# Value shifts issued by SP and subtracted by VectorE, and a first normalization applied by a diagonal matrix, in a hybrid transformer kernel

## The chip, the cores and the metric

One core of one Trainium2 chip runs the whole kernel as one program. The metric is the device time of one execution in microseconds (us), the median of three runs.

## The reference, cut to what matters

The reference is two transformer layers one after the other on x of 512 tokens by 1024 features, all in float32. What the change touches is the start of the first layer and the values of its stick-breaking attention:

```python
def hybrid_layer(x, norm_pre, w_in, ...):
    h = rmsnorm(x, norm_pre)                      # x * rsqrt(mean(x*x) + EPS) * norm_pre
    proj = jnp.einsum('bld,de->ble', h, w_in)
    z_ssd, xbc, dt_raw, q, k, v, z_sb, gates = jnp.split(proj, _split_points(), axis=-1)
    # xbc: causal convolution of 4 taps, silu; dt: softplus; then ssd_scan (chunked scan)
    # y: gated group rmsnorm with z_ssd
    o = stick_breaking(q, k, v)                   # causal, 16 heads of 64
    ...

# stick_breaking, per block of queries
log_fail = jnp.where(mask, jax.nn.log_sigmoid(-logits), 0.0)
between = lax.cumsum(log_fail, axis=3, reverse=True) - log_fail
w = jnp.where(mask, jnp.exp(jax.nn.log_sigmoid(logits) + between), 0.0)
outs.append(jnp.einsum('bhqk,bkhd->bqhd', w, v[:, :kend]))
```

The second layer (sparse attention, a gated linear recurrence, a feed-forward network) follows and is not touched. The kernel doesn't form w itself: a reverse scan on VectorE gives running sums of weights, and these are multiplied with the steps of the values, v[t] - v[t-1], which gives the same output.

## The kernel before, in words

Tokens lie in four tiles of 128 (index t, `NT`), features in eight chunks of 128 (index k, `NK`). Every large product runs as three float32r products (high half of the weights times high half of the activations, and the two mixed ones). Weights come in blocks of up to 128x2048, each in two pieces of 128x1024 that SP loads (L699) into two buffers `wraw`; ScalarE rounds a piece to `whi` (`round_weights`, L1150), VectorE subtracts to get `wlo` (`rest_of_weights`, L1485). SP loads piece i of block n when `wlo` of piece i of block n-1 is done (L697). Every function of TensorE ends in `mm`, recorded as L744; transposes against the identity are recorded at their own lines.

`plan()` writes one list of steps, `STEPS`, and every engine walks it in that order and does its share of each step. So a wait of one instruction holds up everything behind it on that engine. Each block is a run of eight `gemm` steps; ScalarE rounds the next block's pieces at steps 0 and 2, VectorE makes the rests at steps 2 and 4.

**The start.** SP loads the four tiles of x (L692), the constants `cst` with the identity (L690) and, spread over all partitions, the weights `norm_pre` (L691). For each tile ScalarE squares and sums (`norm`, L1263), VectorE makes mean and reciprocal (L1637, L1638), ScalarE takes the root (`root`, L1244), VectorE multiplies the tile by its factor and `norm_pre` (`apply`, L1648), TensorE turns it in two halves of four transposes (`turn`, L807), ScalarE rounds each half out of PSUM into `a_hi` (L1267) and VectorE writes the rest to `a_lo` (L1680). Then comes the small product for dt (`small_block`, 16 products with `sw`), for which all splits must be done, and block 0 of the projection. The first block needs `whi` (L1150) and `wlo` (L1485) of its first piece; both engines make them after the last split of x.

**The convolution.** Blocks 0 to 5 give the twelve tiles of xbc. For each tile VectorE does four convolution instructions (`conv`, L1502 and L1504 three times) and a product (`silu`, L1515). Step `ssd_decay` comes after block 2: TensorE sums decays (two products of `stat` and `cst`), VectorE reads them (L1852 to L1856) and only then has TensorE a free bank for the next transposes (`xturn`, L1008). POOL begins that step with the zeroing of `rounded_arena` (L2011, 128x1024; it reads the identity, times 0.0), which VectorE waits for only at step `stack`, and then does `decays(0)` and `decays(1)` (two L2003 each), which wait for dt.

**The values.** Blocks v to v+3 (so the four value blocks are called here) give v in two halves of 512 features. When the last token tile of a half is summed, ScalarE copies it out (L1224) and issues three DMAs on its own queue (L1229 to L1231, 896 KB, 120 KB and 6 KB) that copy the half, shifted by one token, into `v_before`. POOL then subtracts (L2056, 128x2048) once for each half. In between the same two engines turn and round y for the group norm (steps `norm`, `apply` L1652, `turn` L807 and L1267 for y), which is woven into blocks v to v+2. Blocks v+4 and v+5 are the first two gate blocks; into these and the fourteen that follow the 64 units of stick-breaking are woven, one per `gemm` step. Unit u: logits on TensorE, two sigmoids on ScalarE (L1291, L1292), the scan on VectorE (L1926); two units later the transposes (L1085) and their copy (L1301), three later the product with the value steps (`bank<-arena`). The first unit's sigmoid waits for the first half of the steps (`s_dv` 1), heads from 8 on and the first `y_ssd` tile (L1543) for the second (`s_dv` 2).

The lines of the old value path:

```python
act.wait_ge(s_vz, half + 1)
act.dma_start(v_before[half][1:113, :, :], vt[0:112, :, cols]).then_inc(s_vs[half], 16)
act.dma_start(v_before[half][113:P, :, :], vt[112:P - 1, :, cols]).then_inc(s_vs[half], 16)
act.dma_start(v_before[half][0:1, 1:NT, :], vt[P - 1:P, 0:NT - 1, cols]).then_inc(s_vs[half], 16)
```

Of the kernel before, what the change touches and what calls it, by code (L numbers as in the profile page):

```python
# [23 lines left out]
ALU = mybir.AluOpType  # L24
# [7 lines left out]
P = 128  # L32
T = 512
D = 1024
# [46 lines left out]
def plan():  # L81
# [52 lines left out]
    for row in normed(["x"], gap=1):  # L134
        steps += row[::-1] if row[-1][0] != "turn" else row
# [118 lines left out]
def plan_tiles():  # L254
# [3 lines left out]
    for s in STEPS:  # L258
        if s[0] == "gemm":
            begun += opened(BLOCKS[s[1]], s[2])  # L260
            done += closed(BLOCKS[s[1]], s[2])
            ended += closed(BLOCKS[s[1]], s[2])
        elif s[0] in ("turn", "small", "smallturn", "qkturn", "level", "hout"):
# [18 lines left out]
    groups = {"turn": (4, 6, 7), "dt": (7,), "level": (2, 3), "hout": (2, 3), "turn_qk": (2, 3), "hq": (0, 1), "hf": (0, 1),  # L282
# [46 lines left out]
FILLS = {"x": "A", "y": "B", "mix": "A", "hgrn": "B", "ffn": "A"}  # L329
ROWS = {"x": "norm_pre", "y": "ssd_norm", "mix": "norm_mix", "ffn": "norm_ffn"}  # L330
# [8 lines left out]
def plan_splits():  # L339
# [9 lines left out]
    for s in STEPS:  # L349
        if s[0] == "turn":  # L350
            done(s, FILLS[s[1]], range(4 * s[3], 4 * s[3] + 4), [s[2]])
        if s[0] == "merge":
# [34 lines left out]
CST = Columns([("ident", P), ("tri", P), ("ones", P)])  # L387
# [16 lines left out]
TURNS = [s for s in SPLITS if s[0] in ("turn", "nsa")]  # L404


def block_of(kind):
    return min(n for n, b in enumerate(BLOCKS) if TILES[b["tiles"][0]][0] == kind)

# [11 lines left out]
def emit(nc, dram, spill, out):  # L421
    ctx = ExitStack()
    with ctx:
# [84 lines left out]
        vt = mem(32, [NT, D])  # L508
        junks = {"x": mem(0, [NT, D]), "y": mem(60, [2, 512])}
        rows = {"x": mem(64, [D]), "y": mem(48, [D]), "mix": mem(80, [D]), "ffn": mem(0, [D])}  # L510
# [100 lines left out]
        s_vz, s_dv = sem("s_before_first_zero"), sem("s_value_steps")  # L611
# [6 lines left out]
        s_out = sem("s_stored")  # L618
        s_hid4, s_hidz = sem("s_hidden_repeated"), sem("s_hidden_zero")
# [66 lines left out]
        def _(sp):  # L686
            by_token = lambda ap: ap.rearrange("(a p) d -> p a d", p=P)
            for t in range(NT):
                if t == 2:
                    sp.dma_start(cst[:, :], dram["cst"]).then_inc(s_ident, 16)  # L690
                    sp.dma_start(rows["x"], dram["norm_pre"]).then_inc(s_row["x"], 16)  # L691
                sp.dma_start(xt[:, t, :], by_token(dram["x"])[:, t, :]).then_inc(s_x[t], 16)  # L692
            sp.dma_start(swraw[:, 0:NK * SH], dram["w_dt"]).then_inc(s_sw, 16)
            for n in range(NB):
                for i in range(2):
# [3 lines left out]
                    sp.dma_start(wraw[i][:, 0:cols.stop - cols.start], dram["wblk"][n][:, cols]).then_inc(s_w[i], 16)  # L699
                if n == 1:  # L700
# [41 lines left out]
        def _(pe):  # L742
# [56 lines left out]
            def turn(name, t, half, g):  # L799
                src = {"x": xt, "y": xs, "mix": xn, "hgrn": mixt, "ffn": xn}[name]  # L800
# [1335 lines left out]
```

## Time and profile before

| | before |
|---|---|
| median of 3 runs | 1460.55 us (1459.8 to 1462.16) |
| profiled execution, its own time | 1462.84 us |
| its span | 1461.0 us |
| TensorE busy | 1390.3 us (95%) |
| VectorE busy | 757.8 us (52%) |
| ScalarE busy | 582.6 us (40%) |
| GpSimd busy | 121.2 us (8%) |
| mean DMA rate | 83 GB/s |
| mean granted TensorE clock | 0.985 |

The span is the time from the first to the last recorded instruction; 1.84 us lie around it. Busy time of overlapping matmuls is counted once. The chain that ended last lies on TensorE for 82%, on VectorE for 10% and on ScalarE for 4% of the span. A duration behind "xN" is that of N instructions together, so their pitch is that time divided by N.

### The profile page before, as it was taken

How to read it: one execution, taken by the hardware profiler on the slowest of the kernel's cores; microseconds unless marked ns; L12 is line 12 of the kernel's file. 1: busy time of each engine (PE TensorE's matmuls, PEld its weight loads, DVE VectorE, ACT ScalarE, POOL GpSimd, SP SyncE). 2: the span in 40 equal slices, each digit the busy share in tenths (PEclk: the TensorE clock that was granted, in tenths of full speed). 3: DMA queues.
4: the chain of work that ended last, by engine and by line, in shares of the span. 5: the costliest groups of instructions: out<-in, count | busy, mean ns of one | idle time of the engine just before them, and what ended most of it. 6: DMA issues, size and time to landing. Idle time of an engine off the chain costs nothing.

```text
span 1461.0 us, 17660 instructions
## 1 busy us (share of the span) xinstructions
PE 1390.3 (95%) x6909; PEld 1133.9 (78%) x6913; DVE 757.8 (52%) x1148; ACT 582.6 (40%) x1061; POOL 121.2 (8%) x87
## 2 busy tenths in 40 slices
PE   6899999998999999998899989999979999999999
PEld 4787778876888888876787767767868888888887
DVE  4775554555666553334554757557643433443443
ACT  4534333446777532234425444542332322322221
POOL 0107430011000000000000122221000000000000
PEclk9999999999999999999999999999999999999999
DMA  4221222332111254222431100000512233223322
GB/s 156 74 85 58 76 69 84 104 115 58 59 58 45 79 179 140 92 95 73 151 103 58 44 15 29 15 16 15 173 58 87 88 101 100 92 97 100 100 88 101
DMA packets 35493, 121.78 MB, mean 83 GB/s; under 512 B 3924, under 2 KB 5204, under 8 KB 35154
## 3 DMA queue, kind: packets, MB, share of 16 engines
q1 hardware_dynamic: 33744, 117.50, 24.0%
q10 hardware_dynamic: 1666, 3.14, 0.8%
q8 instruction: 56, 0.92, 0.2%
q14 instruction: 27, 0.22, 0.0%
HBM read 113.29 MB, written 4.19 MB: 80 GB/s over the span
## 4 chain that ended last, share of the span: by engine, by line
PE 82%; DVE 10%; ACT 4%; issue 2%; ACTq 1%; DMA 1%; POOL 0%; SPq 0%; DVEq 0%
PE bank L744 79%; PE bank L1085 1%; PE bank L906 1%; PE bank L807 1%; DVE wlo L1485 1%; DVE arena L1504 1%; ACT arena L1263 1%; DMA arena<-in_x 1%; ACT whi L1150 0%; DVE arena L1779 0%; DVE arena L1655 0%; DVE arena L1810 0%; ACT a_hi L1267 0%; DVE arena L1784 0%; DVE a_lo L1680 0%
## 5 line engine op out<-in xcount | busy, mean ns | idle before, releaser
L744 PE MATMUL bank<-a_hi,whi 128*128 128x512 f32 x848 | 342.2, 404 | 1.5 <-DVE arena L1933 0.9
L744 PE MATMUL bank<-a_hi,wlo 128*128 128x512 f32 x848 | 332.7, 392 | 0.0
L744 PE MATMUL bank<-a_lo,whi 128*128 128x512 f32 x848 | 332.3, 392 | 0.0
L1485 DVE TENSOR_TENSOR wlo<-wraw,whi 128x1024 fp32r<-128x1024 f32 x194 | 248.6, 1293 | 54.5 <-ACT whi L1150 49.1
L1150 ACT ACTIVATE whi<-wraw 128x1024 fp32r<-128x1024 f32 x194 | 196.9, 1044 | 183.2 <-PE bank L744 177.1
L744 PE MATMUL bank<-arena 128*128 128x128 f32 (+7 forms) x1400 | 221.0, 304 | 9.0 <-DVE arena L1784 4.9
L744 PEld LDWEIGHTS bank<-arena 128*128 128x128 f32 (+2 forms) x1400 | 175.4, 190 | 36.6 <-issue 21.3
L744 PEld LDWEIGHTS bank<-a_hi,wlo 128*128 128x128 f32 x848 | 160.4, 189 | 34.6
L744 PEld LDWEIGHTS bank<-a_hi,whi 128*128 128x128 f32 x848 | 160.8, 190 | 33.9 <-issue 2.0
L744 PEld LDWEIGHTS bank<-a_lo,whi 128*128 128x128 f32 x848 | 160.9, 190 | 31.9 <-issue 1.0
L744 PE MATMUL bank<-whi,a_hi 128*128 128x512 f32 x320 | 127.8, 400 | 6.9 <-DVE a_lo L1680 3.9
L744 PE MATMUL bank<-whi,a_lo 128*128 128x512 f32 x320 | 125.7, 393 | 0.0
L744 PE MATMUL bank<-wlo,a_hi 128*128 128x512 f32 x320 | 125.5, 392 | 0.0
L744 PE MATMUL bank<-whi,b_hi 128*128 128x512 f32 x240 | 94.5, 394 | 0.0
L744 PE MATMUL bank<-whi,b_lo 128*128 128x512 f32 x240 | 94.1, 392 | 0.0
L744 PE MATMUL bank<-wlo,b_hi 128*128 128x512 f32 x240 | 93.9, 391 | 0.0
L1926 DVE TENSOR_TENSOR_SCAN arena<-arena 128x128 f32<-128x128 f32 (+1 forms) x64 | 56.7, 888 | 67.1 <-ACT arena L1292 66.8
L744 PEld LDWEIGHTS bank<-whi,a_hi 128*128 128x128 f32 x320 | 60.6, 190 | 19.9 <-issue 7.7
L1199 ACT ACTIVATE b_hi<-arena 128x512 fp32r<-128x512 f32 x30 | 19.0, 632 | 135.6 <-DVE arena L1590 123.7
L744 PEld LDWEIGHTS bank<-whi,a_lo 128*128 128x128 f32 x320 | 60.6, 189 | 12.9
L744 PEld LDWEIGHTS bank<-wlo,a_hi 128*128 128x128 f32 x320 | 60.7, 190 | 11.9
L1580 DVE TENSOR_TENSOR arena<-arena,bank 128x512 f32<-128x512 f32 x32 | 22.0, 688 | 92.1 <-PE bank L744 92.1
(235 smaller groups left out, 1671.5 us busy)
## 6 DMA issues: line engine op xcount, KB each, us to landing
wraw<-in_wblk SPq DMA_DIRECT2D x190, 512.0 KB, 3.7
arena<-in_x SPq DMA_DIRECT2D x4, 512.0 KB, 6.0
arena<-in_x SPq DMA_DIRECT2D x1, 2048.0 KB, 8.3
spill<-arena SPq DMA_DIRECT2D x4, 512.0 KB, 6.6
arena<-spill SPq DMA_DIRECT2D x1, 2048.0 KB, 9.4
out<-arena SPq DMA_DIRECT2D x8, 256.0 KB, 2.6
arena<-arena ACTq DMA_DIRECT2D x2, 896.0 KB
arena<-in_w1k SPq DMA_DIRECT2D x1, 1024.0 KB, 7.1
```

The costliest lines, as they stand in the source:

```text
L744: return nc.tensor.matmul(o, lhsT, rhs, start=start, stop=stop, **kw)
L807: last = nc.tensor.transpose(bank[BANK[g]][:, P * i:P * i + P], src[:, t, c0 + P * i:c0 + P * i + P], ident)
L906: last = nc.tensor.transpose(bank[BANK_WT][:, o:o + P], np_[v % 3][:, b_, P * kb:P * kb + P], ident)
L1085: last = nc.tensor.transpose(bank[BANK_WT][:, P * kb:P * kb + P], sb_w[:, v % 3, P * kb:P * kb + P], ident)
L1150: A(whi[n % 2][:, cols], wraw[i][:, 0:cols.stop - cols.start], ACT.Copy).then_inc(s_hi, 1)
L1199: A(b_hi[:, c, :], tt[:, p % 2, :], ACT.Copy).then_inc(s_tround, 1)
L1263: A(junk[:, t, :], src[:, t, :], ACT.Square, accum_out=nss[name][:, t:t + 1]).then_inc(s_ss, 1)
L1485: v.tensor_tensor(wlo[n % 2][:, cols], wraw[i][:, 0:cols.stop - cols.start], f32(whi[n % 2][:, cols]), ALU.subtract).then_inc(s_lo, 1)
L1504: ins = v.scalar_tensor_tensor(acc[:, j:T], x_[:, 0:T - j], V("conv_w", 4 * i + 3 - j), acc[:, j:T], ALU.mult, ALU.add)
L1580: v.tensor_tensor(x, x, ps[:, :], ALU.add).then_inc(s_end["V"], 1)
L1926: v.tensor_tensor_scan(w[:, ::-1], fail[:, ::-1], sig[:, ::-1], 0.0, ALU.mult, ALU.add)\
```

## The change

At the start: `norm_pre` comes as eight columns of `cst`, which is loaded second. VectorE writes `diag`, the identity times the token factors of a tile (128x128), in place of the scaled tile. TensorE multiplies each 128x128 chunk of the raw x by `diag` as an ordinary float32 product (`feed`, eight a tile), which turns and scales it at once, into eight banks, one per feature chunk. After the fourth tile, ScalarE and VectorE split whole chunks of 128x512 (step `chunk`), with `norm_pre` as scale per partition. `small_block` waits chunk by chunk. Before all that, TensorE does 14 products of a constant, and ScalarE takes a root of a constant. On POOL, `decays(0)` comes before the zeroing. In the value path SP issues the shifting DMAs, between the two pieces of blocks v+4 (first half) and v+5 (second half), and VectorE subtracts in four instructions of 128x512 for each half: the first half at step `stack`, the second one by one in units 4 to 7. Cut to its core:

```diff
-    for row in normed(["x"], gap=1):
-        steps += row[::-1] if row[-1][0] != "turn" else row
+    chunks = [tile("x_t", c) for c in range(NK)]
+    for t in range(NT):
+        steps += [("norm", "x", t), ("apply", "x", t), ("feed", t)]
+    steps += [("chunk", c, g) for c, g in enumerate(chunks)]
...
-            need[s[:2]] = max(v for (x, _, _), v in last.items() if x == "A")
+            for k in range(NK):
+                need[(*s[:2], k)] = max(last["A", t, k] for t in range(NT))
...
-CST = Columns([("ident", P), ("tri", P), ("ones", P)])
+CST = Columns([("ident", P), ("tri", P), ("ones", P), ("norm_pre", NK)])
+WARMING = 14
+SHIFTS = [block_of("v") + 4, block_of("v") + 5]
...
             for t in range(NT):
-                if t == 2:
+                if t == 1:
                     sp.dma_start(cst[:, :], dram["cst"]).then_inc(s_ident, 16)
-                    sp.dma_start(rows["x"], dram["norm_pre"]).then_inc(s_row["x"], 16)
...
+                    if i == 0 and n in SHIFTS:
+                        half = SHIFTS.index(n)
+                        src, dst = vt[:, :, 512 * half:512 * half + 512], v_before[half]
+                        sp.wait_ge(*ended(tile_of("v", (NT - 1, half))))
+                        sp.wait_ge(s_y, NT)
+                        if half == 1:
+                            sp.wait_ge(s_split, max(SPLITS.index(x) for x in SPLITS if x[:2] == ("turn", "y")) + 1)
+                        sp.dma_start(dst[1:113, :, :], src[0:112, :, :]).then_inc(s_vs[half], 16)
+                        sp.dma_start(dst[113:P, :, :], src[112:P - 1, :, :]).then_inc(s_vs[half], 16)
+                        sp.dma_start(dst[0:1, 1:NT, :], src[P - 1:P, 0:NT - 1, :]).then_inc(s_vs[half], 16)
...
+            def feed(t):
+                if t == 0:
+                    pe.wait_ge(s_warm, 1)
+                    for _ in range(WARMING):
+                        mm(bank[NK - 1][:, T - P:T], warm, warm, True, True)
+                pe.wait_ge(s_norm, norm_no("x", t))
+                for c in range(NK):
+                    last = mm(bank[c][:, P * t:P * t + P], xt[:, t, P * c:P * c + P], diag[:, t, :], True, True)
+                    if t == NT - 1:
+                        last.then_inc(s_tile, 1)
...
-                need_split(SPLIT_NEED["small", kind])
                 for k in range(NK):
+                    need_split(SPLIT_NEED["small", kind, k])
...
-                    if t == NT - 1:
-                        ... (the three act.dma_start of before, with their waits)
...
+            act.wait_ge(s_unit, 1)
+            A(unit_root, unit, ACT.Sqrt)
             for s in STEPS:
-                if s == ("apply", "x", NT - 1):
+                if s == ("chunk", 0, tile_of("x_t", 0)):
                     round_small("dt")
...
+                if s[0] == "chunk":
+                    c, g = s[1:]
+                    act.wait_ge(s_tile, DONE[g])
+                    A(a_hi[:, c, :], bank[BANK[g]][:, :], ACT.Copy, scale=cst[:, CST.at("norm_pre")][:, c:c + 1]).then_inc(s_round, 1)
...
-                    last = v.scalar_tensor_tensor(xt[:, t, :], xt[:, t, :], r, rows["x"], ALU.mult, ALU.mult)
+                    dve.wait_ge(s_ident, 16)
+                    last = v.tensor_scalar(diag[:, t, :], ident, r, None, ALU.mult)
...
+            def steps_of_values(half, t):
+                cols = slice(512 * half, 512 * half + 512)
+                dve.wait_ge(s_vs[half], 48)
+                ins = v.tensor_tensor(vt[:, t, cols], vt[:, t, cols], v_before[half][:, t, :], ALU.subtract)
+                if t == NT - 1:
+                    ins.then_inc(s_dv, 1)
             def stick(u):
+                if NT <= u < 2 * NT:
+                    steps_of_values(1, u - NT)
...
+            v.memset(unit, 1.0).then_inc(s_unit, 1)
+            v.memset(warm, 1.0).then_inc(s_warm, 1)
             for s in STEPS:
+                if s[0] == "chunk":
+                    c, g = s[1:]
+                    dve.wait_ge(s_round, TURNS.index(s) + 1)
+                    v.scalar_tensor_tensor(a_lo[:, c, :], bank[BANK[g]][:, :], cst[:, CST.at("norm_pre")][:, c:c + 1],
+                                           f32(a_hi[:, c, :]), ALU.mult, ALU.subtract).then_inc(s_split, 1)
...
+                    for half in range(2):
+                        link(v.memset(v_before[half][0:1, 0, :], 0.0))
+                    for t in range(NT):
+                        steps_of_values(0, t)
...
                 if s[0] == "ssd_decay":
+                    decays(0)
                     pool.wait_ge(s_ident, 16)
                     g_.tensor_scalar(mem(92, [2 * NT, P], rounded_arena), ident.unsqueeze(1).to_broadcast([P, 2 * NT, P]), 0.0, None,
                                      ALU.mult).then_inc(s_kz, 1)
-                    decays(0)
...
-                if s[0] == "stack":
-                    ... (POOL's memsets of v_before and its two subtractions, L2052 and L2056)
```

## Rows read from the trace of the kernel before

**Rows 1.** Busy time in stretches: stretch, length, busy of each engine, PEclk, DMA

```profile
62.00:74.00 12.00, 6.83 (x26) 5.53 (x26) 7.10 (x14) 5.92 (x10) 0.00 (x0) 0.72 0.23 72
...
326.00:347.00 21.00, 14.06 (x59) 10.74 (x59) 11.78 (x10) 11.16 (x22) 4.52 (x1) 0.84 0.35 101
```

**Rows 2.** Timeline of ScalarE at the start: start, duration, instruction, idle before

```profile
4.48 1.06 ACT L1263 ACTIVATE arena<-arena 128x1024 f32<-128x1024 f32 x1 [2.46 <-DMA arena<-in_x]
...
6.92 1.28 ACT L1244 ACT_TABLE_LOAD   x1
...
9.97 1.06 ACT L1263 ACTIVATE arena<-arena 128x1024 f32<-128x1024 f32 x1 [1.55 <-DMA arena<-in_x]
...
20.50 1.99 ACT L1150 ACTIVATE whi<-wraw 128x1024 fp32r<-128x1024 f32 x2
```

**Rows 3.** Timeline of VectorE at the start

```profile
8.77 1.29 DVE L1648 SCALAR_TENSOR_TENSOR arena<-arena,stat 128x1024 f32<-128x1024 f32 x1 [1.49 <-DMA arena<-in_norm_pre]
...
21.58 2.36 DVE L1485 TENSOR_TENSOR wlo<-wraw,whi 128x1024 fp32r<-128x1024 f32 x2 [0.25 <-ACT whi L1150]
```

**Rows 4.** Timeline of TensorE at the start

```profile
10.11 1.97 PE L807 MATMUL bank<-cst,arena 128*128 128x128 f32 x8 [10.11 <-DVE arena L1648]
...
27.03 0.40 PE L744 MATMUL bank<-a_hi,whi 128*128 128x512 f32 x1
```

**Rows 5.** Timeline of GpSimd: the zeroing, and the second subtraction

```profile
6.61 2.77 POOL L2011 TENSOR_SCALAR rounded_arena<-cst 128x1024 fp32r<-128x1024 f32 x1 [6.17 <-DMA cst<-in_cst]
...
335.14 4.52 POOL L2056 TENSOR_TENSOR arena<-arena 128x2048 f32<-128x2048 f32 x1 [14.24 <-DMA arena<-arena]
```

**Rows 6.** Timeline of TensorE after the stall at 62.8 us

```profile
67.99 1.08 PE L1008 MATMUL bank<-cst,arena 128*128 128x128 f32 x4 [5.17 <-DVEq L1856]
```

**Rows 7.** Timeline of VectorE in the convolution, beside GpSimd's products and after them

```profile
53.15 4.30 DVE L1504 SCALAR_TENSOR_TENSOR arena<-arena,vec 128x511 f32<-128x511 f32 x3
...
59.68 2.33 DVE L1504 SCALAR_TENSOR_TENSOR arena<-arena,vec 128x511 f32<-128x511 f32 x3
```

**Rows 8.** Timeline of ScalarE and its queue around the two halves of the values

```profile
303.94 1.57 ACTq L1231 DMA_DIRECT2D arena<-arena  x1
...
328.98 1.95 ACTq L1231 DMA_DIRECT2D arena<-arena  x1
...
332.63 0.28 ACT L1291 ACTIVATE arena<-bank 128x128 f32<-128x128 f32 x1
...
337.73 1.06 ACT L1150 ACTIVATE whi<-wraw 128x1024 fp32r<-128x1024 f32 x1
```

**Rows 9.** Timeline of TensorE around the values and the first units

```profile
311.90 0.66 PE L807 MATMUL bank<-cst,arena 128*128 128x128 f32 x4 [1.75 <-DVE arena L1652]
...
340.26 0.69 PE L1085 MATMUL bank<-cst,arena 128*128 128x128 f32 x2 [4.05 <-DVE arena L1926]
...
345.54 0.77 PE L744 MATMUL bank<-b_hi,whi 128*128 128x512 f32 x1
...
350.73 1.06 PE L744 MATMUL bank<-arena 128*128 128x128 f32 x8
351.54 0.48 PE L744 MATMUL bank<-b_hi,whi 128*128 128x512 f32 x1
```

**Rows 10.** Timeline of VectorE around the values and the first units

```profile
299.08 1.41 DVE L1652 SCALAR_TENSOR_TENSOR arena<-arena,stat 128x512 f32<-128x512 f32 x2 [1.22 <-ACT stat L1244]
...
316.97 5.02 DVE L1485 TENSOR_TENSOR wlo<-wraw,whi 128x1024 fp32r<-128x1024 f32 x1 [1.23 <-ACT whi L1150]
...
335.39 5.67 DVE L1926 TENSOR_TENSOR_SCAN arena<-arena 128x256 f32<-128x256 f32 x2 [0.94 <-ACT arena L1292]
```

**Rows 11.** SP's weight loads before unit 0, and their time to landing

```profile
322.02 3.99 SPq L699 DMA_DIRECT2D wraw<-in_wblk  x2
...
DMA to landing us min/median/max: 3.0/3.7/9.8
```

**Rows 12.** DMA queues from 326 to 346 us: packets, MB, share

```profile
q10 hardware_dynamic: 545, 1.05, 20.2%
```

More of the change, by code:

```diff
@@ L262, in plan_tiles @@
             ended += closed(BLOCKS[s[1]], s[2])
+        elif s == ("feed", 0):
+            begun += [g for g, (kind, _) in enumerate(TILES) if kind == "x_t"]
+        elif s[0] == "chunk":
+            done.append(s[2])
+            end[s[2]] = ("split", s)
         elif s[0] in ("turn", "small", "smallturn", "qkturn", "level", "hout"):
@@ L280, in plan_tiles @@
     bank, before = {}, {}
-    groups = {"turn": (4, 6, 7), "dt": (7,), "level": (2, 3), "hout": (2, 3), "turn_qk": (2, 3), "hq": (0, 1), "hf": (0, 1),
+    groups = {"x_t": (0, 1, 2, 3, 4, 5, 6, 7), "turn": (4, 6, 7), "dt": (7,), "level": (2, 3), "hout": (2, 3), "turn_qk": (2, 3), "hq": (0, 1), "hf": (0, 1),
               "gate": (0, 1, 2), "y_ssd": (0, 1, 2)}
@@ L351, in plan_splits @@
             done(s, FILLS[s[1]], range(4 * s[3], 4 * s[3] + 4), [s[2]])
-        if s[0] == "merge":
+        if s[0] in ("merge", "chunk"):
             done(s, "A", [s[1]])
@@ L403 @@
 MERGE_AFTER = max(n for n, b in enumerate(BLOCKS) if b["w"] == "gate_sb")
-TURNS = [s for s in SPLITS if s[0] in ("turn", "nsa")]
+TURNS = [s for s in SPLITS if s[0] in ("turn", "nsa", "chunk")]
 def block_of(kind):
     return min(n for n, b in enumerate(BLOCKS) if TILES[b["tiles"][0]][0] == kind)
+SHIFTS = [block_of("v") + 4, block_of("v") + 5]
 def end_of(kind, i=None):
@@ L508, in emit @@
         vt = mem(32, [NT, D])
+        diag = mem(64, [NT, P])
+        warm = mem(66, [P])
+        unit, unit_root = stat[:, STAT - 2:STAT - 1], stat[:, STAT - 1:STAT]
         junks = {"x": mem(0, [NT, D]), "y": mem(60, [2, 512])}
-        rows = {"x": mem(64, [D]), "y": mem(48, [D]), "mix": mem(80, [D]), "ffn": mem(0, [D])}
+        rows = {"y": mem(48, [D]), "mix": mem(80, [D]), "ffn": mem(0, [D])}
         craw = mem(0, [2, T])
@@ L1105, in _ @@
                     turn(*s[1:])
+                if s[0] == "feed":
+                    feed(s[1])
                 if s[0] == "small":
@@ L2092, in lay_out @@
     cst[:, CST.at("ones")] = 1.0
+    cst[:, CST.at("norm_pre")] = cols(norm_pre[0])
     bf = mybir.dt.np(BF16)
@@ L2118, in lay_out @@
             "w1v": w1(cmp_v_w1_2), "cst2": cst2, "upto": upto, "cmask": cmask.reshape(P, P),
-            "halves": halves.reshape(P, 6 * 256), "onorm": rows(hgrn_o_norm_2[0]), "norm_pre": rows(norm_pre[0]),
+            "halves": halves.reshape(P, 6 * 256), "onorm": rows(hgrn_o_norm_2[0]),
             "ssd_norm": rows(ssd_norm[0]), "norm_mix": rows(norm_mix_2[0]), "norm_ffn": rows(norm_ffn_2[0])}
```

30 lines of the change are left out of this document (6 added, 24 removed).

## The prediction, made before the changed kernel was run

> **What bounds the kernel now.** I read the chain of waits first: it lies on TensorE nearly throughout, so only stretches in which TensorE waits can give time back. The waits listed by engine and the busy time by stretch then show where: 10.11 us before its first transposes [rows 4] and the slow build-up behind them; a stall at 62.8 us, where it is busy for 6.83 of 12 us; and 326 to 347 us, where it is busy for 14.06 of 21 us at a mean clock of 0.84 [rows 1]. The timelines of each engine in those three places do the rest. Everything between is matmul after matmul, and a shift of its start shifts it whole. Sums stand against one profiled execution (1462.84 us, span 1461.0); the median is 2.29 us lower, and I take the differences over to it.
>
> **The start.** Before, ScalarE squares the first tile at 4.48, loads the root's table for 1.28 us at 6.92 and waits 1.55 us for the third tile, whose data comes behind 512 KB of `norm_pre` [rows 2]. Block 0 starts at 27.03 [rows 4], because after the last split of x come the small products, and because TensorE worked at the lower level: eight transposes took 1.97 us, 0.25 each, where four at granted clock 1.00 later took 0.66, 0.17 with their tail [rows 4, 9].
>
> After, step by step. A tile costs ScalarE square (1.06), reading the sum (about 0.1 more), VectorE's two short instructions and the root (estimated together 0.6 with their hand-overs from the spacing of this timeline), so 1.8 us. The table load goes before the data: 0 on the path. The 512 KB row transfer goes too: between the landings of the first and third tile, 4.48 and 9.97 [rows 2], came 0.2 MB of `cst` and three times 0.52 MB, so 0.32 MB/us, and 0.52 MB are 1.6 us: the third tile is there at 8.4. So factors are ready at 6.3, 8.1, 10.2 and 12.0; `diag` of 128x128 adds an estimated 0.25 us, which is 1.29/8 for an eighth of L1648's elements [rows 3] and 0.1 of fixed part (bounds 0.1 and 0.4). Feeds: a float32 product of 128x128 is two records; x8 took 0.81 us from its start to the next start (350.73 to 351.54 [rows 9]), so 0.20 us a product and 1.6 us a tile at the upper level, 3.2 us at the lower. Fourteen products of the constant from about 1.1 us last 5.6 us at the lower level, to 6.7, just when the first `diag` is there: they cost 0 or a few tenths, and their cover is the wait for x. I take the upper level for the feeds, as TensorE has then worked for over 5 us, while after the stall at 68 it was back up by the end of the stretch at mean 0.72 [rows 1]. Last feed 12.35 to 14.0, first chunk at 12.6. Then eight chunks: ScalarE 0.5 each, VectorE's scalar_tensor_tensor 1.41/2 = 0.70 each [rows 10]: it bounds, from 13.2 to 18.8. The 16 small products run in its shadow, two a chunk. `wlo` of piece one takes 2.36/2 = 1.18 [rows 3], so block 0 starts at 20.0 in place of 27.03: **gain 7.0**. Were TensorE at the lower level throughout, feeds would end at 19.9, the chunks at 21.4, the small products (0.40 each) at 25: gain 2. Both ends are kept.
>
> The Trainium skill (TensorE: Matmul & The Clock Gate, Terms) says that transpose mode is 4x faster for FP32 than a plain product. The rows at the upper level give at most 0.17 for a transpose and 0.20 for a product, so this trace disagrees; by the page a feed would take 8 x 4 x 0.11 = 3.5 us by estimate, block 0 would start about 3 us later, and this gain would be 4.
>
> **POOL's order.** `decays(0)` and (1) slow VectorE: three convolution instructions took 4.30 us beside them and 2.33 alone [rows 7]. That lag ends in TensorE's 5.17 us wait at 67.99 for VectorE's read of the decays [rows 6], since VectorE has no gap between. The zeroing took 2.77 us at 6.61 [rows 5], away from all that; now it runs between `decays(0)` and (1), inside this stretch. Waiting for it: `decays(1)` behind it on POOL (not needed before the scan's second unit, far later), and VectorE only at `stack`. Its price is what it takes from VectorE. Lower end 0: VectorE's L1648 started at 8.77, while the zeroing ran until 9.38, and took 1.29 for 1024 elements [rows 3, 5], no more for each than L1652 far from any GpSimd work, 0.70 for 512 [rows 10]. Upper end: all 2.77 us. The nearest row is the same instruction beside the same kind of VectorE work, but it shows only 0.6 of the 2.77 us; I **charge 0.7**.
>
> The Trainium skill (SBUF — State Buffer, Who interferes with whom) says that a VectorE instruction with two SBUF inputs contends with a GpSimd instruction that reads SBUF, and the second fully blocks. By it L1648 should have stretched by 0.6 us, which the row doesn't show; by it the price here would be near 2.8.
>
> **The values, first half.** ScalarE's three issues end at 303.94 + 1.57 = 305.51 [rows 8], 3.8 us after they began. Behind them stand the copy of a y turn, two roundings and the squares of the last y tile, so VectorE's L1652 is late and TensorE waits 1.75 us at 311.90 [rows 9]. Without them all of that comes 3.8 us earlier: **gain 1.75**, the clock was 1.00 and gives nothing. SP issues these DMAs after the `wlo` rest of block v+3's first piece, about 305, with 0.4 to 2 us each as on ScalarE's queue; behind them on SP only the second piece of v+4 waits, about 3 us, and it has over 10. POOL's first subtraction blocked VectorE's L1485 for 5.02 instead of 1.2 [rows 10], but 9 us before use: nothing.
>
> **The values, second half, and the first units.** Before: last value copy ends 327.3; three issues until 330.93 [rows 8]; table load; first sigmoid 332.63 [rows 8]. Then the scans of units 1 and 2 take 5.67 us beside POOL's second subtraction, which alone lasts 4.52 [rows 5, 10], and TensorE waits 4.05 at 340.26 and works at the lower level until about 346 [rows 9].
>
> After: VectorE at `stack` adds two tiny memsets and four subtractions at 1.18/2 = 0.6 each, about 3.1 us from about 324.4, where the timeline has its last work of that step, ending at 327.5; ScalarE's table load ends at 328.6 and hides them. If that cover went they would cost as much as they last past it. First sigmoid 328.65, 4.0 earlier. The same ladder of ScalarE that took 332.63 to 337.73 [rows 8] then asks for the second piece of block v+5 at 333.75. That is the new wait. SP now holds that load: it waits for the last value tile (327.3) and issues the shifts for 3.6 us, so the load goes out at 331.0, where it went at 322.02 + 3.99 - 0.33 = 325.7 [rows 11]. With a landing time of 3.7 [rows 11], and behind 1.05 MB of shifts [rows 12], I put it at 334.8. Queued behind that rounding are unit 3's sigmoids and unit 1's copy; TensorE waits for them at unit 4, some 2 us. VectorE's four subtractions of the second half, 0.6 each in units 4 to 7, fall into gaps of about 1 us a unit. TensorE starts unit 4's block step at 338.2 where it did at 345.54 [rows 9]: **gain 7.3**. Ends: without any wait its work from 327.5 takes about 8 us, 335.4, gain 10.1; if the piece lands 4 us later than I put it, 3.3.
>
> **Sum.** 7.0 + 1.75 + 7.3 - 0.7 = 15.35 us. Profiled execution 1447.5, median 1460.55 - 15.35 = **1445.2**. The dropped ACT, POOL and DMA work elsewhere hides behind TensorE and is worth nothing.
>
> **Rivals.**
> (a) The start gives little: TensorE isn't brought up, or the feeds run at the lower level, or a product costs the page's ratio. For it: no row shows what wakes the engine from the very start. Against: 5.6 us of products. Gain 2 to 4 in place of 7: 1449 to 1450.
> (b) The zeroing blocks VectorE whole, and `decays(1)` collides later as before: 2.1 us more than charged, 1447.3. The page's rule above speaks for it, the row at 8.77 against it.
> (c) SP becomes the bound at v+5: the piece lands 4 us later, so unit 3 and all behind it wait, and the clock stays down as it did for the 5 us before 346: 1449 to 1451, and 1452 with (b).
> (d) Slower than before: the same place, but SP's chain goes wrong by more. SP holds all loads in order; while it waits for the last value tile and issues, block v+5's second piece and all of v+6 stand behind it. From 15.35 us of further delay past 334.8, which is a landing after 350, the whole gain is gone and with 4 more us the time is 1464.5. For it: issues on this path took up to 1.95 us [rows 8] and landing up to 9.8 [rows 11]. Against: even these together give 5 us.
> (e) TensorE has no stall to give back, since VectorE or ScalarE's own ladder takes the place: start 2, values 1, zeroing 2.8 lost: 1460.
>
> **Chances.** Forecast 0.50, better than it (no waits in the units, gain up to 10) 0.12, (a) 0.14, (b) 0.10, (c) 0.08, (e) 0.04, (d) 0.02. Their times lie from about 1440.5 to 1452 but for the last two, so the range is **1440.5 to 1452**: at best 1445.2 - 2.8 (no wait in the units) - 0.7 (zeroing free) - 1 (start), at worst (a) or (c) together with (b). A measurement here can tell 0.2%, 2.9 us, from no change. Faster by more: 0.94; within: 0.04; slower: 0.02.
>
> **What the changed profile would show.** Right: block 0's first product near 20.0; feeds of 1.6 us; no table load between squares and root; VectorE's convolution near 47 to 53 longer by under 1 us and TensorE's wait at the decays 5 to 6 us; no wait above 0.5 us at the y turns; scans without POOL beside them; one wait of about 2 us near unit 4, released by ScalarE and behind it by a load of SP. Wrong: feeds of 3 us, a decay wait near 8 us, or a load of v+5 landing more than 10 us after the last value copy.

## The result and the profile after

The changed kernel takes 1449.21 us (median of 4 runs, 1447.66 to 1450.59) against 1461.36 us (4 runs, 1459.8 to 1462.55): ratio 0.9917, 95% interval 0.9900 to 0.9934, so 12.1 us or 0.83% faster. In a second set on another chip it took 1449.36 against 1461.59 us, ratio 0.9918 (0.9903 to 0.9933). The forecast was 1445.2 us in a range of 1440.5 to 1452. Each experiment below but the last two is a single execution, and executions of one kernel lie up to 3.5 us apart. The profiled execution took 1450.34 us with a span of 1448.5.

Line numbers moved: TensorE's `mm` is now L769, the squares L1293, the roots L1274, `diag` L1685, the chunk's two halves L1446 and L1987, `wlo` L1521, the convolution L1538 and L1540, `xturn` L1043, the shifts L722 to L724, the value steps L1954, the sigmoids L1321 and L1322, the scan L1972.

Busy time of the changed kernel in the three places (stretch, length, PE, PEld, DVE, ACT, POOL, PEclk, DMA; compare [rows 1]):

```profile
0.00:30.00 30.00, 27.43 (x147) 21.41 (x148) 12.49 (x28) 16.69 (x29) 0.20 (x4) 1.00 0.49 168
...
54.00:66.00 12.00, 5.94 (x28) 4.96 (x27) 9.08 (x17) 5.25 (x10) 0.55 (x1) 0.79 0.31 88
...
318.00:335.00 17.00, 13.67 (x78) 10.90 (x77) 12.66 (x20) 11.70 (x25) 0.00 (x0) 1.00 0.42 124
```

The stretch at the decays is no better than before (5.94 us busy of 12, where it was 6.83). The units' stretch is 17 us in place of 21, with the clock at 1.00 in place of 0.84.

The start, ScalarE (answers to [rows 2]):

```profile
0.73 1.28 ACT L1403 ACT_TABLE_LOAD   x1 [0.73 <-PEq L2173]
...
4.71 1.06 ACT L1293 ACTIVATE arena<-arena 128x1024 f32<-128x1024 f32 x1 [2.48 <-DMA arena<-in_x]
...
7.46 1.06 ACT L1293 ACTIVATE arena<-arena 128x1024 f32<-128x1024 f32 x1 [0.99 <-DMA arena<-in_x]
...
9.14 1.04 ACT L1293 ACTIVATE arena<-arena 128x1024 f32<-128x1024 f32 x1
...
10.80 1.04 ACT L1293 ACTIVATE arena<-arena 128x1024 f32<-128x1024 f32 x1
```

Now the second tile is the one waited for (7.46 us); the third and fourth are not. From there a tile costs 1.66 us. TensorE, same stretch (answers to [rows 4]):

```profile
1.08 7.82 PE L769 MATMUL bank<-arena 128*128 128x128 f32 x44 [1.08 <-DVE arena L1982]
9.61 5.62 PE L769 MATMUL bank<-arena 128*128 128x128 f32 x48 [0.70 <-DVE arena L1685]
...
21.22 0.47 PE L769 MATMUL bank<-a_hi,whi 128*128 128x512 f32 x1 [0.53 <-issue]
```

The first row holds the 14 products of the constant (28 records) and the first feed (16), the second the other three feeds, which run back to back: their 24 products start between 9.61 and 14.96, 0.22 us each, so a feed takes 1.8 us. Block 0 starts at 21.22 in place of 27.03.

The convolution beside GpSimd (VectorE, then GpSimd; answers to [rows 5, 7]):

```profile
47.43 3.64 DVE L1540 SCALAR_TENSOR_TENSOR arena<-arena,vec 128x511 f32<-128x511 f32 x3
...
51.59 2.06 DVE L1521 TENSOR_TENSOR wlo<-wraw,whi 128x1024 fp32r<-128x1024 f32 x1
53.58 1.26 DVE L1538 TENSOR_SCALAR arena<-arena,vec 128x512 f32<-128x512 f32 x1
```

```profile
48.27 3.21 POOL L2069 TENSOR_SCALAR rounded_arena<-cst 128x1024 fp32r<-128x1024 f32 x1
51.45 1.12 POOL L2060 TENSOR_TENSOR b_hi<-cst,b_hi 128x512 fp32r<-128x512 f32 x1
```

TensorE's longest waits in all of the changed kernel (who, for whom, total, times, longest; the second answers to [rows 6]):

```profile
PE bank L830 <- DVE arena L1692: 13.3, 5, 5.4
PE bank L1043 <- DVEq L1893: 6.1, 1, 6.1
```

The first units: ScalarE, then TensorE (answer to [rows 8, 9]):

```profile
321.33 1.28 ACT L1321 ACT_TABLE_LOAD   x1 [1.00 <-DVE arena L1954]
322.62 0.28 ACT L1321 ACTIVATE arena<-bank 128x128 f32<-128x128 f32 x1
...
329.05 1.06 ACT L1187 ACTIVATE whi<-wraw 128x1024 fp32r<-128x1024 f32 x1 [1.34 <-DMA wraw<-in_wblk]
```

```profile
327.85 0.41 PE L1120 MATMUL bank<-cst,arena 128*128 128x128 f32 x2 [1.15 <-DVE arena L1972]
...
331.49 0.52 PE L1120 MATMUL bank<-cst,arena 128*128 128x128 f32 x3 [1.29 <-ACT arena L1331]
...
332.21 0.48 PE L769 MATMUL bank<-b_hi,whi 128*128 128x512 f32 x1
```

Five marks on TensorE split the 12.5 us by which the span fell. They are used for all experiments: block 0's first product; the first `xturn` behind the decay wait; unit 0's first logits product; unit 4's block step; the end.

| | before | after | gained |
|---|---|---|---|
| start to block 0 | 27.03 | 21.22 | 5.8 |
| to the end of the decay wait | 40.96 | 41.95 | -1.0 |
| to unit 0 | 259.55 | 257.41 | 2.1 |
| to unit 4's block step | 18.00 | 11.63 | 6.4 |
| to the end | 1115.5 | 1116.3 | -0.8 |

### The profile page after: what moved, and what is told of

Same layout as the page of the kernel before. It is cut to its first block, busy times and chain, and to the rows that moved or that the text cites. A ratio compares the mean times of both kernels' runs of the same rounds, so it can differ in the third digit from the quotient of the medians.

```text
span 1448.5 us, 17782 instructions
## 1 busy us (share of the span) xinstructions
PE 1393.3 (96%) x6969; PEld 1138.4 (79%) x6973; DVE 753.4 (52%) x1160; ACT 581.5 (40%) x1061; POOL 111.6 (8%) x83
## 4 chain that ended last, share of the span: by engine, by line
PE 85%; DVE 8%; ACT 3%; issue 2%; DMA 1%; SPq 0%; DVEq 0%; ACTq 0%
PE bank L769 82%; PE bank L1120 1%; PE bank L941 1%; PE bank L830 1%; DVE wlo L1521 1%; ACT arena L1293 0%; DVE arena L1816 0%; DVE arena L1847 0%; DMA arena<-in_x 0%; DVE arena L1692 0%; DMA wraw<-in_wblk 0%; DVE arena L1821 0%; DVE arena L1826 0%; ACT whi L1187 0%; PE bank L1043 0%
## 5 line engine op out<-in xcount | busy, mean ns | idle before, releaser
L769 PE MATMUL bank<-a_hi,whi 128*128 128x512 f32 x848 | 341.9, 403 | 2.1 <-DVE arena L1979 0.9
L769 PE MATMUL bank<-a_hi,wlo 128*128 128x512 f32 x848 | 332.6, 392 | 0.0
L769 PE MATMUL bank<-a_lo,whi 128*128 128x512 f32 x848 | 332.0, 392 | 0.0
L1521 DVE TENSOR_TENSOR wlo<-wraw,whi 128x1024 fp32r<-128x1024 f32 x194 | 245.6, 1278 | 55.0 <-ACT whi L1187 49.6
L769 PE MATMUL bank<-arena 128*128 128x128 f32 (+8 forms) x1492 | 232.4, 303 | 10.8 <-DVE arena L1821 4.9
L769 PEld LDWEIGHTS bank<-arena 128*128 128x128 f32 (+2 forms) x1492 | 186.4, 191 | 38.8 <-issue 21.3
L769 PEld LDWEIGHTS bank<-a_hi,whi 128*128 128x128 f32 x848 | 160.7, 190 | 34.6 <-ACT whi L1187 2.0
L769 PEld LDWEIGHTS bank<-a_hi,wlo 128*128 128x128 f32 x848 | 160.1, 189 | 34.4
L769 PEld LDWEIGHTS bank<-a_lo,whi 128*128 128x128 f32 x848 | 160.7, 189 | 31.6 <-issue 1.0
L769 PE MATMUL bank<-whi,a_hi 128*128 128x512 f32 x320 | 128.5, 402 | 7.0 <-DVE a_lo L1717 3.9
L769 PE MATMUL bank<-whi,a_lo 128*128 128x512 f32 x320 | 126.5, 395 | 0.0
L769 PE MATMUL bank<-wlo,a_hi 128*128 128x512 f32 x320 | 126.2, 394 | 0.0
L769 PE MATMUL bank<-whi,b_hi 128*128 128x512 f32 x240 | 94.9, 395 | 0.0
L769 PE MATMUL bank<-whi,b_lo 128*128 128x512 f32 x240 | 94.2, 393 | 0.0
L769 PE MATMUL bank<-wlo,b_hi 128*128 128x512 f32 x240 | 94.2, 392 | 0.0
L1972 DVE TENSOR_TENSOR_SCAN arena<-arena 128x128 f32<-128x128 f32 (+1 forms) x64 | 52.7, 823 | 58.4 <-ACT arena L1322 58.2
L769 PEld LDWEIGHTS bank<-whi,a_hi 128*128 128x128 f32 x320 | 61.1, 191 | 20.0 <-issue 7.8
L769 PEld LDWEIGHTS bank<-whi,a_lo 128*128 128x128 f32 x320 | 60.9, 190 | 13.1
L769 PEld LDWEIGHTS bank<-wlo,a_hi 128*128 128x128 f32 x320 | 61.2, 191 | 12.1
```

The source lines that it names most:

```text
L769: return nc.tensor.matmul(o, lhsT, rhs, start=start, stop=stop, **kw)
L1521: v.tensor_tensor(wlo[n % 2][:, cols], wraw[i][:, 0:cols.stop - cols.start], f32(whi[n % 2][:, cols]), ALU.subtract).then_inc(s_lo, 1)
L1972: v.tensor_tensor_scan(w[:, ::-1], fail[:, ::-1], sig[:, ::-1], 0.0, ALU.mult, ALU.add)\
```

## The experiments

Traces are compared by these marks, since a single time scatters by about 1.5 us for the reason given further down. The marks scatter too: where the start is the changed kernel's, with the same loads in the same order, block 0 begins between 20.73 and 21.86 us (8 traces), because the second tile of x lands at different times. Experiments start from the changed kernel unless another is named. The expectations of experiments 1 and 2 count 19.3 and 12.9 us to unit 4's block step from the last value product, which starts 1.3 us before the mark at unit 0 (18.0 and 11.6).

**1. The value path alone, on the kernel before.**

```diff
 (kernel before)
+ SHIFTS, SP's block of waits and three dma_start, steps_of_values on VectorE
- the three act.dma_start, GpSimd's memsets and subtractions
```

> The kernel before with the value path alone changed (SP issues the shifts, VectorE subtracts). Theory, that the change is three separate gains which add up: block 0 stays at 27.0 us, TensorE's wait at the y turns (1.75 us) goes, and from the last value product to unit 4's block step it is 12.9 us as in the changed kernel, not 19.3; in all 8.3 us shorter, span near 1452.7. Rival, that the value path gains less at the old, slower start because the waits are where they are for other reasons: under 6 us.

Measured: 1452.75 us beside 1459.96, span 1451.0. Block 0 at 27.20, decay wait 5.16; from block 0 to unit 0 298.8 us instead of 300.5; to unit 4's block step 11.43 instead of 18.00. The gain up to that step is 8.1 us, where the theory has 8.3; the rival is out.

**2. The start alone** (the old value path and GpSimd's old order).

```diff
-                    decays(0)                      # ahead of the zeroing
+                    decays(0)                      # behind it, as before
- SP's shifts, VectorE's steps_of_values
+ the three act.dma_start, GpSimd's memsets and subtractions
```

> The changed kernel with the old value path (ScalarE issues, GpSimd subtracts) and GpSimd's old order. Theory of separate gains: block 0 at 21.2 us, the wait for the decays back near 5.2, the whole 5.8 us shorter, span near 1455.2, with the y wait of 1.75 us and 19.3 us up to unit 4's block step back. Rival, that part of the 5.8 us is lost again in the convolution whatever GpSimd does: the products after the decay wait come only 4.8 us early.

Measured: 1456.73 us, span 1454.9. Block 0 at 20.73, decay wait 5.20 with its end at 61.75, 6.24 us earlier than before: nothing is lost in the convolution, so the rival is out. The y wait is back (1.60 us), as is the long wait for the scans (3.60 us) and 16.6 us up to unit 4's block step. Two sizes missed: the start gains 6.3 us here and not 5.8, as the second tile came early (its squares at 6.73), and the last stretch is 1.4 us shorter than the 18.0 expected. TensorE was at the lower level for a shorter part of it: the granted clock was 0.82, 0.50 and 0.83 in the three stretches of 2 us from 332 us on, where the kernel before had 0.89, 0.50, 0.50 and 0.50 in the four from 338 us on.

**3. GpSimd's order alone undone.**

```diff
                 if s[0] == "ssd_decay":
-                    decays(0)
                     pool.wait_ge(s_ident, 16)
                     g_.tensor_scalar(...).then_inc(s_kz, 1)
+                    decays(0)
```

> The changed kernel with the zeroing ahead of decays(0) on GpSimd, as before. Theory, that the zeroing between the decays takes about 1 us from VectorE: the wait at the decays falls from 6.1 to 5.2 us and the products behind it start 1 us earlier, 62.2 instead of 63.2; if it now collides with VectorE's small work on diag at 6 to 9 us, block 0 moves by at most 0.3. Rival, that the extra wait comes from VectorE's own order after the faster start: it stays at 6 us.

VectorE and GpSimd of this kernel:

```profile
47.48 4.30 DVE L1540 SCALAR_TENSOR_TENSOR arena<-arena,vec 128x511 f32<-128x511 f32 x3
51.70 0.68 DVE L1551 TENSOR_TENSOR arena<-arena 128x512 f32<-128x512 f32 x1
52.30 1.21 DVE L1521 TENSOR_TENSOR wlo<-wraw,whi 128x1024 fp32r<-128x1024 f32 x1
```

```profile
5.30 2.77 POOL L2068 TENSOR_SCALAR rounded_arena<-cst 128x1024 fp32r<-128x1024 f32 x1 [4.86 <-DMA cst<-in_cst]
```

The decay wait is 5.17 us, and its end comes 41.04 us after block 0 instead of 41.95: 0.9 us. Block 0 stays (21.27). The zeroing between the decays costs 0.9 us of its 3.2. The rows say where. In the changed kernel the second of the three convolution instructions, started 0.6 us into the zeroing, took 1.41 us, and the third, started 2.1 us into it, 0.75 (alone each takes 0.75, beside the decays 1.41). That is 0.66 us. The rest is that `decays(1)`, pushed back, slows the weights' rest (2.06 for 1.21 us) and the next convolution instruction (1.26 for 0.53) in place of two convolution instructions. The single time of 1449.95 us shows nothing of it.

**4. Only the issuing back on ScalarE; 5. only the subtracting back on GpSimd.**

```diff
 (4) - SP's waits and three dma_start     + the three act.dma_start
 (5) - steps_of_values, VectorE's memsets + GpSimd's memsets and subtractions
```

> The changed kernel with the shifting DMAs issued by ScalarE again; VectorE subtracts. Theory, that issuing and subtracting each have their own price: the y wait of 1.75 us returns, the first sigmoid comes about 2 us later than in the changed kernel, since 3.6 us of issuing replace 1.6 us of waiting for the subtractions, and ScalarE's 1.34 us wait for the second piece of block v+5 goes; in all 3 to 4 us longer than the changed kernel. Rival, that the collision of GpSimd with the scans was the whole of it: no more than 2 us longer.

> The changed kernel with both subtractions (and the clearing of the first row) back on GpSimd; SP issues. Theory: the first sigmoid comes earlier than in the changed kernel by the 1 us that ScalarE waits there for VectorE; but the second subtraction then runs beside scans 1 to 3 and blocks VectorE for about 4 us, and TensorE's granted clock falls again. Unit 4's block step 3 to 5 us later. Rival, that the issues were the price and GpSimd's subtraction is harmless when it comes early: equal within 1 us.

| from unit 0 to unit 4's block step | VectorE subtracts | GpSimd subtracts |
|---|---|---|
| SP issues | 11.6 (after) | 12.3 (5) |
| ScalarE issues | 14.6 (4) | 16.6 (2), 18.0 (before) |

In (4) the y wait is back at 1.72 us, and the first sigmoid comes at 326.70, so 5.0 us after unit 0's logits product against 2.0 in the changed kernel. The mark at unit 4 comes 4.1 us later than in the changed kernel, the end of this one execution (1451.89 us) 2.7 us later. So issuing on ScalarE brings back the y wait of 1.7 us and lengthens the units by 3.0 us, and the first theory holds in its parts. Not all of the 3.0 is issuing: TensorE now waits 1.8 and 1.6 us there and then works at the lower level, which the changed kernel doesn't (the granted clock, third number from the right, is 0.61 and 0.54 where the changed kernel has 1.00):

```profile
332.00:334.00 2.00, 2.00 (x8) 1.70 (x9) 1.75 (x3) 2.00 (x4) 0.00 (x0) 0.61 0.13 16
334.00:336.00 2.00, 2.00 (x10) 1.73 (x9) 1.68 (x2) 0.94 (x4) 0.00 (x0) 0.54 0.74 240
```

By estimate from these two rows, (0.39 + 0.46) x 2 us, up to 1.7 us of the 3.0 is clock. In (5), 1452.1 us, the second subtraction does collide:

```profile
329.39 4.83 POOL L2108 TENSOR_TENSOR arena<-arena 128x2048 f32<-128x2048 f32 x1 [12.45 <-DMA arena<-arena]
```

```profile
332.30 3.33 DVE L1970 TENSOR_TENSOR_SCAN arena<-arena 128x512 f32<-128x512 f32 x2 [2.46 <-ACT arena L1322]
```

(the two scans take 1.65 us without it), but now at units 3 and 4, and unit 4's block step comes 0.6 us later after unit 0, not 3 to 5. That expectation missed, and the number is the rival's (equal within 1 us), though the subtraction was not harmless to VectorE: with early issues it meets a stretch in which TensorE waits for a weight piece anyway (2.2 us in one piece, with the granted clock at 0.65 and 0.50 in the two stretches of 2 us from 332 us on). What it costs behind that mark was not taken apart.

**6. No products of the constant.** The 14 products are left out (their result is never used).

```diff
-WARMING = 14
+WARMING = 0
```

> The changed kernel without the 14 products of a constant. They are 0 of the output. Theory, that they bring the feeds to the upper level: without them the first feeds take 3.2 us instead of 1.6 and TensorE, working from 6.8 us on, comes up during the second or third; the last feed then ends 0 to 2.5 us later, and block 0 starts up to 2 us later. Rival, that the 14 products give nothing, since the feeds wait for factors and the chunks are bound by VectorE: block 0 within 0.3 us of 21.2. Second rival, that they are in the way (the first feed starts late in the changed kernel): block 0 earlier.

TensorE, the four feeds:

```profile
6.67 9.42 PE L769 MATMUL bank<-arena 128*128 128x128 f32 x64 [6.67 <-DVE arena L1685]
```

From 6.67 to 10.86 us a record starts every 0.21 us, from 11.02 us on every 0.11, as in the changed kernel from 6.5 us on. The slower figure is double the other, which is the ratio of the two levels, 1.2 and 2.4 GHz; the granted clock in the profile says 1.00 in both, so in the first microseconds it has to be read from the pitch. The last tile's squares start 0.1 us later than in the changed kernel, the first chunk's copy at 14.57 in place of 13.71: the products give 0.75 us. Block 0 at 22.08 is above all traces with the products, if by only 0.2 us above the latest of them, whose second tile came 0.5 us later than here; both rivals are out.

**7. The root's table loaded late.**

```diff
-            act.wait_ge(s_unit, 1)
-            A(unit_root, unit, ACT.Sqrt)
```

> The changed kernel without the root of a constant at the start, so the root's table is loaded between the first squares and the first root. Theory: the load of 1.28 us falls into ScalarE's 0.99 us wait for the second tile of x, so it costs only about 0.5 us at block 0. Rival, that the load is on the path in full: block 0 1.3 us later.

```profile
5.51 1.28 ACT L1274 ACT_TABLE_LOAD   x1
6.92 1.04 ACT L1293 ACTIVATE arena<-arena 128x1024 f32<-128x1024 f32 x1
```

Block 0 at 20.79, 0.4 us earlier than in the changed kernel, time 1447.35. The load lies in the wait for the second tile, which happened to land by 6.92 here; in nine traces with the constants ahead of it and the early load its squares started between 6.73 and 8.09, eight of them at 7.42 or later. So the whole start tells nothing of the load's price, and both expectations missed. The rows tell a little: the load puts the first `diag` at 7.05 where it came at 6.51, the four feeds then run back to back from 7.39,

```profile
7.39 7.41 PE L769 MATMUL bank<-arena 128*128 128x128 f32 x64 [0.21 <-DVE arena L1683]
```

and the last of them starts 0.3 us after its `diag` is there. In this order of loads the early root is worth a few tenths at most. In the order of experiment 8, where the second tile's squares start at 6.05, the load would end at 6.8 by this trace; that was not run.

**8. The constants behind the second tile.**

```diff
-                if t == 1:
+                if t == 2:
                     sp.dma_start(cst[:, :], dram["cst"]).then_inc(s_ident, 16)
```

> The changed kernel with the constants loaded third, behind the second tile of x, in place of second. Theory, that block 0 is late against the forecast because the second tile lands at 7.5 to 8.1 us behind the constants: its squares start near 6.3 to 6.9 and block 0 starts 0.5 to 1 us earlier, while the first feed, which now waits for the identity, still ends before the second diag is ready. Rival, that the third and fourth tile bound it then: block 0 within 0.3 us of 21.2.

```profile
6.05 1.04 ACT L1293 ACTIVATE arena<-arena 128x1024 f32<-128x1024 f32 x1
8.37 1.06 ACT L1293 ACTIVATE arena<-arena 128x1024 f32<-128x1024 f32 x1 [0.57 <-DMA arena<-in_x]
```

The second tile isn't waited for any more, the third comes at 8.37, and block 0 starts at 20.34: 0.9 us earlier than in the changed kernel's first trace and 0.4 us earlier than in the best of the eight traces with its order. Time 1448.95.

**9. The second shift behind the second piece of block v+5.**

```diff
-                    if i == 0 and n in SHIFTS:
+                    if (n, i) in ((SHIFTS[0], 0), (SHIFTS[1], 1)):
```

> The changed kernel with the second half's shift issued after the second piece of block v+5 in place of before it. Theory: ScalarE's 1.34 us wait for that piece goes, and TensorE's 1.29 us wait at unit 4 with it; the shifts land before VectorE's unit 4, so unit 4's block step starts 1 to 1.5 us earlier. Rival, that VectorE waits at unit 4 for the shifts instead: nothing gained, or up to 1 us lost.

```profile
328.01 1.06 ACT L1187 ACTIVATE whi<-wraw 128x1024 fp32r<-128x1024 f32 x1
```

```profile
331.76 0.69 DVE L1954 TENSOR_TENSOR arena<-arena 128x512 f32<-128x512 f32 x1 [0.46 <-DMA arena<-arena]
```

ScalarE's wait and TensorE's at unit 4 are gone, VectorE waits 0.46 us for the shift, and the mark is at 10.32 instead of 11.63: 1.3 us, with the granted clock at 1.00 in both. Time 1447.0.

**10. The units' tables and rows ready.**

```diff
+  (ScalarE, unit 0) A(unit_root, unit, ACT.Sigmoid)   # ahead of its waits
-  (VectorE) link(v.memset(v_before[half][0:1, 0, :], 0.0))
+  (GpSimd) the same two memsets, early; VectorE waits for them
```

> The changed kernel with the first rows of v_before cleared by GpSimd early, and with a sigmoid of a constant on ScalarE ahead of its wait for the first value steps. Theory, that the table load of 1.28 us sits behind a wait of 1.0 us that hides nothing and that the two clearings with their hand-overs (1.28 us) make VectorE late: the first sigmoid comes 1.0 us after the last value copy starts to be free, about 1.3 to 1.6 us earlier than in the changed kernel. TensorE then still waits for the second piece of block v+5, so unit 4's block step moves by 0.3 us at most. Rival, that the first sigmoid alone sets it: unit 4 earlier by over 1 us.

The first sigmoid comes 1.17 us after unit 0's logits product instead of 2.04. But all of it, and more, goes into the next wait:

```profile
329.50 1.06 ACT L1187 ACTIVATE whi<-wraw 128x1024 fp32r<-128x1024 f32 x1 [2.16 <-DMA wraw<-in_wblk]
```

```profile
331.95 0.87 PE L1120 MATMUL bank<-cst,arena 128*128 128x128 f32 x3 [2.11 <-ACT arena L1333]
...
334.32 0.63 PE L769 MATMUL bank<-b_hi,wlo 128*128 128x512 f32 x1
```

Two waits of 1.15 and 1.29 us became one of 2.11, after which the products run at 0.43 us spacing in place of 0.23, the lower level, for some 3 us. Unit 4's block step is 0.6 us later (12.22), which neither the theory (0.3 us earlier at most) nor the rival had; the clock was left out of both. 1451.13 us.

**11 and 12. All mended, beside the changed kernel.** Experiments 3, 8, 9 and 10 together, and the changed kernel unedited.

> The changed kernel with four things mended: the zeroing ahead of decays(0), the second shift behind the second piece of block v+5, the constants behind the second tile of x, the first rows cleared by GpSimd and the sigmoid's table loaded ahead of the wait. Theory, that the losses are separate: 0.9 + 1.0 + 0.6 + 1.3 us, so 3 to 4 us under the changed kernel, near 1445.5. Rival, that the waits are shared and the last one stays: under 1.5 us.

> The changed kernel itself, unedited, beside the one with all four mended and on the same chip. Both theories: 1449.2 us, 0.8% under the kernel before. From the first units on its products take between 1113 and 1117 us in the traces so far, by how often the granted clock falls at short waits, so its times spread by some 3 us.

1444.28 us (4 runs, 1443.65 to 1446.08), ratio to the kernel before 0.9884 (0.9868 to 0.9901); the changed kernel beside it 1449.36, 0.9918 (0.9903 to 0.9933). The intervals just don't overlap: by the medians the mended one is 5.1 us faster than the changed kernel, more than the 3 to 4 expected, and 17.3 us faster than the kernel before. Up to unit 4's block step its trace is 4.1 us ahead of the changed kernel's first one (328.15 against 332.21) and 3.7 us ahead of that of experiment 12 (331.81); what is over lies behind that step, in the stretch that scatters. The 4.1 are 0.9 at the decays, 2.2 in the units, where no wait above 0.3 us is left after unit 0's logits, 0.9 between them, and only 0.1 at the start. The 0.9 between them belong to no edit but to the clock: in the 6 us behind the decay wait the granted clock was 0.61 in the changed kernel and 0.77 here, and a difference of 0.16 over 6 us is 1.0 us.

```profile
63.17:69.17 6.00, 6.00 (x19) 4.95 (x20) 1.45 (x2) 3.50 (x7) 0.00 (x0) 0.61 0.15 51
```

```profile
62.21:68.21 6.00, 6.00 (x23) 5.06 (x24) 1.45 (x2) 3.50 (x7) 0.00 (x0) 0.77 0.15 47
```

At the start the zeroing met the first `diag`. VectorE, GpSimd and TensorE:

```profile
6.61 1.09 DVE L1687 TENSOR_SCALAR arena<-cst,stat 128x128 f32<-128x128 f32 x1 [0.65 <-DMA cst<-in_cst]
```

```profile
6.58 2.83 POOL L2069 TENSOR_SCALAR rounded_arena<-cst 128x1024 fp32r<-128x1024 f32 x1 [6.14 <-DMA cst<-in_cst]
```

```profile
7.75 7.41 PE L769 MATMUL bank<-arena 128*128 128x128 f32 x64 [0.49 <-DVE arena L1687]
```

1.09 us where the three other tiles take 0.29. Both start on the landing of the constants. The four feeds then run back to back from 7.75 (6.74 in experiment 8), so the first one's delay reaches block 0 nearly whole: 21.16 against 20.34. Moving the zeroing to a place where neither stands in its way was not tried.

## Why the prediction was right, and where its sizes were off

The forecast of 15.35 us became 12.1: mechanism, places and order were right, and the range held. The time alone would not say so, since 1449.2 us is also what rivals (a) and (c) gave; it is the marks that rule these two out.

**The start, 7.0 forecast, 5.8 measured.** The term that was mis-sized most is the landing of the tiles. I took 1.6 us off for the row transfer that goes, and checked the third tile; but the change also moves 0.2 MB of constants ahead of the second tile, and I let its factor be ready at 8.1 as if it were there. It was at 9.2, and the two tiles behind it queued on ScalarE, so the last `diag` was ready at 12.9 and not at 12.25. The second term is the feed: I read x8 in 0.81 us as 0.20 us a product, but its eight records start 0.11 us apart, a product takes 0.22 and a feed 1.8 us, not 1.6. That is longer than the 1.66 us a tile, so three feeds back to back end up behind their factors, and the last one starts at 13.3, 0.4 us after its `diag`. Experiment 8 takes the late landing away, and with it most of that queue, and gives 20.34, near the 20.0 of the sum. The other terms held: 1.66 us a tile for 1.8; `diag` 0.29 for 0.25; 0.67 us a chunk (4.69/7) for 0.70. A float32 product's 0.22 us stands against 0.11 for a transpose (in the four at 311.90 [rows 9] each behind the second starts 0.11 us after the one before), so the factor is 2 here and not the four of the Trainium skill (TensorE: Matmul & The Clock Gate, Terms). Rival (a) is out, and experiment 6 shows what it would have cost without the products of the constant: 0.75 us, as TensorE comes up by itself during the feeds, 4.3 us after its first product. The table load was rightly counted as nothing once early, and would have been a few tenths late.

**GpSimd's order, 0.7 forecast, 0.9 measured** (experiment 3), between the bounds of 0 and 2.8. Rival (b), the whole instruction, is out.

**First half, 1.75 forecast.** The wait vanished; it comes back at 1.60 and 1.72 us whenever ScalarE issues (experiments 2 and 4). The table has 2.1 us, 0.3 of them clock. From the decay wait to unit 0 the eleven traces without the y wait take 256.5 to 258.0 us, and this scatter is the time that TensorE stays at the lower level behind the decay wait, 2.8 to 6.0 us. At half the clock, half of that time is lost; with it taken off, the eleven lie between 254.9 and 255.1 us and the three with the y wait at 256.9 and 257.0: the wait is worth 1.8 to 2.1 us.

**Units, 7.3 forecast, 6.4 measured.** Two steps failed by about 1 us each. "Two tiny memsets" took 0.48 us each and 0.16 us of waiting each, so VectorE's last subtraction ended 0.9 us after the last value copy (321.25 against 320.33), not 0.2, and the table load, which I had as the cover, sits behind ScalarE's wait (1.00 us) and not beside it. And the second piece of v+5 landed at 329.05, 5.1 us after its issue and 8.5 us after unit 0's logits, where I had 7.3. Both did less harm than they are long, since the second wait swallows the first, which experiment 10 shows. What I expected there, one wait near unit 4 released by ScalarE with an SP load behind it, stood in the trace at 1.29 us for 2; one of 1.15 us for a scan stood ahead of it. Rivals (c) and (d): SP's queue is the bound at that spot, but by 1.3 us (experiment 9), far from the 15 us that (d) needs.

**The rest.** 0.8 us of the difference lies behind unit 4, where the program is the same. Over the fourteen traces this tail took between 1113.4 and 1117.0 us: the waits in it have nearly the same length (the three longest groups stay at 13 to 15, 4.9 and 4.6 us), but the granted clock falls behind more or fewer of them. In the changed kernel's first trace it was down in seven stretches between 620 and 1090 us, 34 us in all (tail 1116.3), in that of experiment 9 in five, 24 us in all (1114.0). This orders most of the traces but not all (experiment 5: 26 us and 1116.2), so the clock is part of the cause and the rest stays open. I had given such scatter no term; single executions of the same kernel range over 3.5 us, and so can't rank edits of 1 us.

## What to carry to other kernels

When a transfer is moved, recompute the landing of every transfer behind its new place, not only of those behind its old one. Issuing the three DMAs of one partition-shifted half held its queue for 3 to 4 us here, so it belongs on a queue with slack, and there behind whatever is needed soon; a wait for late data in front of an urgent load is a new stall. Of stalls in a row, mend the last one first: shortening an earlier one only lengthened it, and one wait of 2.11 us cost the clock that two of 1.15 and 1.29 us had kept (experiment 10).

## What the runs showed of the hardware that was not expected

The zeroing on GpSimd (one source in SBUF) hindered VectorE only in its first part. VectorE instructions that began 1.3 us or more into it ran at their usual length (L1648 at 8.77 [rows 3, 5]; `diag` at 6.56 in experiment 3, 0.28 us, with the zeroing from 5.30 to 8.07), while one that began 0.03 us after it took 0.8 us longer and one that began 0.6 us into it 0.66 us longer (experiments 11 and 3). That is at odds with the Trainium skill (SBUF — State Buffer, Who interferes with whom), by which the loser is blocked for the whole instruction; GpSimd's 128x2048 subtraction of two SBUF sources, however, did block VectorE to its end [rows 5, 10], as it says, and in experiment 5 even a scan that began 2.9 us into it. Whether the second source makes the difference was not tested.

A float32 product of 128x128 takes 0.22 us at the upper level and a transpose 0.11, so turning by a diagonal matrix costs 0.11 us a chunk more than a transpose, and VectorE writes a `diag` in 0.29 us in place of a scaled tile in 1.29 [rows 3].
